# Hybrid NSA/DSA block on one core: the row factors of attention are turned as a 128x8 tile, stored to memory and read back spread over rows

## The reference

```python
z = rmsnorm(h, norm_mix) @ w_in
y_A = nsa_mixer(q_a, k, v, ...) @ w_branch_nsa     # 8 heads of 64: compressed + selected blocks + sliding window
y_B = dsa_mixer(q_b, k_b, v_b, ...) @ w_branch_dsa # 8 heads of 64: top 256 keys by an indexer
h = h + (sigmoid(g_A) * y_A + sigmoid(g_B) * y_B) @ w_out
h = h + (silu(hn @ w_gate) * (hn @ w_up)) @ w_down ; return rmsnorm(h, norm_final)
```

## Time and profile before

| | us |
|---|---|
| median of three runs (1621.24 to 1624.72) | 1623.87 |
| the profiled execution, its own time | 1621.62 |
| its span, first to last instruction | 1618.8 |
| attention stage, about | 424 to 795 |
| PE busy / DVE / ACT / POOL, of the span | 97% / 71% / 40% / 39% |

### The profile page before, as it was taken

How to read it: one execution, slowest core, us unless ns; L and a number is a source line. 1 busy time by engine, 2 the same in 40 slices (tenths; PEclk the granted TensorE clock), 3 DMA queues, 4 the chain that set the end, 5 groups by cost and what they waited for, 6 DMA issues and landing times.

```text
span 1618.8 us, 24584 instructions
## 1 busy us (share of the span) xinstructions
PE 1573.3 (97%) x9008; PEld 1328.9 (82%) x9008; DVE 1153.6 (71%) x2021; ACT 650.4 (40%) x1269; POOL 637.5 (39%) x442
## 2 busy tenths in 40 slices
PE   6999999999999989999999999999999999999997
PEld 5898888888798878898888887888888888888885
DVE  5745889999555667787675167666777776678978
ACT  5543322121565667766421144322223232344445
POOL 4233664221340144433221217444544544445454
PEclk9999999999999999999999999999999999999998
DMA  7032546321515010010254342333333335474433
GB/s 228 16 93 68 128 113 167 105 85 66 138 66 131 15 53 28 15 40 28 71 167 133 107 162 66 98 98 98 98 98 98 98 104 175 166 271 151 157 109 123
DMA packets 173303, 171.10 MB, mean 106 GB/s; under 512 B 25856, under 2 KB 126208, under 8 KB 173184
## 3 DMA queue, kind: packets, MB, share of 16 engines
q1 hardware_dynamic: 172896, 169.01, 34.5%
q10 hardware_dynamic: 288, 0.52, 0.1%
HBM read 122.04 MB, written 47.45 MB: 105 GB/s over the span
## 4 chain that ended last, share of the span: by engine, by line
PE 57%; DVE 1%; POOL 1%; DMA 0%; issue 0%; ACT 0%; SPq 0%; DVEq 0%; ACTq 0%
PE psA L1662 10%; PE psA L1664 10%; PE psA L1663 10%; PE psT L1664 6%; PE psT L1663 6%; PE psT L1662 6%; PE psT L1669 3%; PE psT L1883 3%; PE psA L1772 1%; PE psA L1773 1%; DMA s<-scratch_gates 0%; DVE merged L2418 0%; POOL h L1267 0%; POOL h L1265 0%; PE psT L1935 0%
## 5 line engine op out<-in xcount | busy, mean ns | idle before, releaser
L447 POOL TENSOR_TENSOR w_lo<-w_raw,w_hi 128x1024 fp32r<-128x1024 f32 (+2 forms) x52 | 120.3, 2315 | 257.8 <-ACT w_hi L442 257.5
L1258 POOL TENSOR_TENSOR w_lo<-w_sum,w_hi 128x1024 fp32r<-128x1024 f32 x44 | 115.4, 2625 | 119.5 <-ACT w_hi L1544 119.5
L1481 ACT ACTIVATE s<-s,nmax 128x640 f32<-128x640 f32 (+7 forms) x192 | 144.0, 752 | 29.6 <-DVE nmax L2360 27.9
L1282 POOL TENSOR_TENSOR w_lo<-act_raw,w_hi 128x512 fp32r<-128x512 f32 x77 | 107.4, 1396 | 104.7 <-ACT w_hi L1572 104.7
L1669 PE MATMUL psT<-ident,s 128*128 128x128 f32 x816 | 120.8, 278 | 0.8 <-ACT s L1481 0.8
L442 ACT CAST w_hi<-w_raw 128x1024 fp32r<-128x1024 f32 (+2 forms) x52 | 52.6, 1015 | 141.9 <-PE psA L1664 81.5
L1669 PEld LDWEIGHTS psT<-ident,s 128*128 128x128 f32 x816 | 94.4, 141 | 17.2 <-issue 7.9
L2450 DVE COPY pT<-psT 128x512 f32<-128x512 f32 (+1 forms) x116 | 69.7, 601 | 53.7 <-PE psT L1669 53.5
L2581 DVE TENSOR_TENSOR w_lo<-wd,w_hi 128x512 fp32r<-128x512 f32 x77 | 90.4, 1177 | 23.9 <-ACT w_hi L1579 23.6
L1572 ACT CAST w_hi<-act_raw 128x512 fp32r<-128x512 f32 x77 | 47.9, 622 | 123.3 <-PE psT L1664 66.4
L2250 DVE TENSOR_SCALAR_CACHE_REDUCE equal<-score,bit_try 128x512 f32<-128x512 f32 (+2 forms) x93 | 93.8, 1008 | 0.0
(11 more groups left out here) (380 smaller groups left out, 4673.7 us busy)
## 6 DMA issues: line engine op xcount, KB each, us to landing
act_raw<-scratch_act SPq DMA_DIRECT2D x77, 256.0 KB, 3.1
w_raw<-in_w_in_dram SPq DMA_DIRECT2D x24, 512.0 KB, 4.0
scratch_act<-act SPq DMA_DIRECT2D x33, 256.0 KB, 2.1
scratch_act<-act_sum SPq DMA_DIRECT2D x33, 256.0 KB, 2.1
wd<-in_w_down_dram SPq DMA_DIRECT2D x33, 256.0 KB, 3.1
scratch_gates<-gate_out SPq DMA_DIRECT2D x32, 256.0 KB, 3.1
gates<-scratch_gates SPq DMA_DIRECT2D x30, 256.0 KB, 4.1
a<-in_w_gate_dram SPq DMA_DIRECT2D x22, 256.0 KB, 3.2
```

The source lines that it names most:

```text
L447: nc.gpsimd.tensor_tensor(lo, raw, hi.bitcast(F32), ALU.subtract).then_inc(self.lo_done, 1)
L1258: nc.gpsimd.tensor_tensor(lo2[n % RING][:], block_of(n)[:], hi2[n % RING][:].bitcast(F32), ALU.subtract)\
L1282: nc.gpsimd.tensor_tensor(lo2[slot][:, 0:512], act_raw[n % 6][:], hi2[slot][:, 0:512].bitcast(F32), ALU.subtract)\
L1481: a_.activation(s_sb[v % SR][:, 0:n], s_sb[v % SR][:, 0:n], ACT.Exp, scale=-1.0, bias=nmax[:, BR[a], i, h:h + 1], accum_out=psum_p[:, BR[a ...
```

## The change

POOL no longer spreads the factors and `r_wide` is gone. DVE multiplies the 128x8 reciprocals by the gate right away (win and slc). PE turns them once at step e+4, as 128x8, to 8 partitions by 128 rows. ACT copies that to `factors_T` at step e+5, issues a store of its 4 KB to memory at e+6, waits for it at e+8, and then issues a read that lays two rows of 2 KB (even heads, odd heads) over 64 partitions each, 128x512 in all, into one of two new tiles. DVE multiplies with that tile at e+12 instead of e+7, and POOL's sum and the later steps move by five as well: `STEPS6` becomes 207, the high parts of the last NSA rows come at `len(units)+12`. In `groups6` the factors' entry comes two steps earlier and is taken out by ACT. The store and the read count on one of two semaphores, used alternately. `O_LAG` stays 6. SP is not touched.

```diff
-    R_LAG = 3
-    O_LAG, F_LAG, Y_LAG = T_LAG + 1 + V_LAG + 1, T_LAG + 1 + V_LAG + 2, 8
+    R_LAG = 4
+    O_LAG, F_LAG, Y_LAG = T_LAG + 1 + V_LAG + 1, T_LAG + 1 + V_LAG + 2 + 5, 8 + 5
...
-        if tile_of(u, O_LAG):
-            groups6.append(("r", *tile_of(u, O_LAG)))
+        if tile_of(u, R_LAG):
+            groups6.append(("r", *tile_of(u, R_LAG)))
...
-        return key[0] in ("ch", "cp") or (key[0] == "p" and key[1] % 2 == 0)
+        return key[0] in ("ch", "cp", "r") or (key[0] == "p" and key[1] % 2 == 0)
...
+    def factors_spilled(t):
+        return spilled[t % 2], spill_count(NT + 4 + t % 2) + 32 * (t // 2) + 16
+    def factors_back(t):
+        return spilled[t % 2], spill_count(NT + 4 + t % 2) + 32 * (t // 2 + 1)
...
# POOL
-            if tile_of(u, R_LAG):
-                a, i = tile_of(u, R_LAG)
...
-                if a == "dsa":
-                    nc.gpsimd.tensor_copy(r_wide[:], r).then_inc(wide_done, 1)
-                else:
...
-                    nc.gpsimd.tensor_tensor(r_wide[:], r, gate, ALU.mult).then_inc(wide_done, 1)
...
-                pool.wait_ge(t_dve, max(dve_took["r", a, i], dve_took["co", i, 0]))
+                pool.wait_ge(scaled_done, t6[a, i] + 1)
+                pool.wait_ge(t_dve, dve_took["co", i, 0])
...
# ACT
+            if tile_of(u - 2, R_LAG):
+                a, i = tile_of(u - 2, R_LAG)
+                t = t6[a, i]
+                act.wait_ge(t_act, act_took["r", a, i])
+                act.dma_start(rD[t].rearrange("r n t -> n r t"), factors_T[:]).then_inc(spilled[t % 2], 16)
+            if tile_of(u - 4, R_LAG):
+                a, i = tile_of(u - 4, R_LAG)
+                t = t6[a, i]
+                if t >= 2:
+                    act.wait_ge(scaled_done, t - 1)
+                act.wait_ge(*factors_spilled(t))
+                act.dma_start(factors[t % 2][:], rD[t].rearrange("r n t -> r (n t)").unsqueeze(1).to_broadcast([2, HD, 4 * P]))\
+                    .then_inc(spilled[t % 2], 16)
...
+            if tile_of(u - 1, R_LAG):
+                a, i = tile_of(u - 1, R_LAG)
+                act.wait_ge(t_ps, g6["r", a, i] + 1)
+                a_.copy(factors_T[:], psT[0:H, g6["r", a, i] % 3, 0:P]).then_inc(t_act, 1)
...
# PE
-            if tile_of(u, O_LAG):
...
-                turn4(group(("r", a, i)), [r_wide[:, 2 * n:2 * n + 2, :].rearrange("p a d -> p (a d)") for n in range(4)])\
-                    .then_inc(t_ps, 1)
+            if tile_of(u, R_LAG):
+                a, i = tile_of(u, R_LAG)
+                pe.wait_ge(rows_done, t6[a, i] + 1)
+                pe.transpose(group(("r", a, i))[0:H, 0:P], psum_r[:, BR[a], i, :], ident[:]).then_inc(t_ps, 1)
...
# DVE
+                branch = 1 if a == "slc" else 2
+                then(v_.reciprocal(r, psum_p[:, BR[a], i, :]))
+                v_.tensor_tensor(r, r, nsa_gate[:, i, H * branch:H * (branch + 1)], ALU.mult).then_inc(rows_done, 1)
...
-            factors = psT[:, g6["r", a, i] % 3, :]
-            dve.wait_ge(t_ps, g6["r", a, i] + 1)
+            wide = factors[t % 2][:]
+            dve.wait_ge(*factors_back(t))
```

More of the change, by code:

```diff
@@ L207, in hybrid_block @@
     yt = sb(work, "ytmp", [P, H * HD])
-    r_wide = sb(work, "row_factors_wide", [P, H, HD])
+    factors_odd = sb(work, "row_factors_odd", [P, 4 * P])
     c_st = sb(work, "c_st", [P, 4, H])
+    factors_T = sb(work, "row_factors_turned", [H, P])
     pg = sb(work, "p_group", [P, KV, 68])
@@ L219, in hybrid_block @@
     psum_r = sb(work, "psum_r", [P, 3, NT, H])
-    sb(work, "skip_merged", [P, HALF + 2 * HALF])
+    factors_even = sb(work, "row_factors_even", [P, 4 * P])
+    sb(work, "skip_merged", [P, 2 * HALF])
     c_s = sb(work, "c_s", [P, H, 64])
@@ L618, in y_ready @@
         if a == "dsa":
[L619 removed]
+            eng.wait_ge(scaled_done, t6[a, i] + 1)
         else:
@@ L650, in hybrid_block @@
     zt_ps, zt_out = sem("zt_ps"), sem("zt_out")
-    spilled = [sem(f"spilled{n}") for n in range(2)]
+    spilled = [sem(f"spilled_or_read_back{n}") for n in range(2)]
     id_ps, relu_done, sc_done = sem("id_ps"), sem("relu"), sem("score_sum")
@@ L698, in hybrid_block @@
     kD = {"slc": scratch["k_slc"], "win": scratch["k_win"]}
-    gD = scratch["gates"]
+    gD, rD = scratch["gates"], scratch["factors"]
+    factors = [factors_even, factors_odd]
+    def factors_spilled(t):
+        return spilled[t % 2], spill_count(NT + 4 + t % 2) + 32 * (t // 2) + 16
+    def factors_back(t):
+        return spilled[t % 2], spill_count(NT + 4 + t % 2) + 32 * (t // 2 + 1)
     hD, aD = scratch["h"], scratch["act"]
@@ L1194, in _ @@
                 n, r = X_AT.index(u) // 2, X_AT.index(u) % 2
-                lows, wides = sum(1 for v in range(u) if y_of(v - 1)), sum(1 for v in range(u) if tile_of(v, R_LAG))
+                lows = sum(1 for v in range(u) if y_of(v - 1))
                 if lows:
                     pool.wait_ge(yl_done, lows)
-                if wides:
-                    pool.wait_ge(wide_done, wides)
                 windows(nc.gpsimd, n, r, (cx_k, cx_v)[n])
@@ L2785 @@
         "q_nsa": (nt, P, 8 * P), "q_dsa": (nt, P, 8 * P), "k_slc": (2, 2, HD, seq), "k_win": (2, 2, HD, seq),
-        "gates": (2 * d // P, P, seq), "h": (nt, P, d),
+        "gates": (2 * d // P, P, seq), "factors": (3 * nt, 2, 4, P), "h": (nt, P, d),
         "act": (7, arrays["w_gate"].shape[2] // (2 * P), P, seq // 2)}.items()}
```

30 lines of the change are left out of this document (12 added, 18 removed).

## The result

| | us |
|---|---|
| before, median of 4 runs (1618.55 to 1624.72) | 1622.55 |
| after, median of 4 runs (1658.39 to 1667.37) | 1662.33 |
| ratio, with its 95% interval | 1.0239 [1.0214, 1.0265] |
| the profiled execution after: own time, span | 1667.37, 1665.6 |

What follows compares the result with a forecast made beforehand. PE, busy 97% of the span, was taken as the bound. Terms -7.5 - 1.3 + 0.5 (ACT) + 6 + 4 + 9.7 + 2.5 = +13.9 us on 1621.6 gave 1635.5, stated as 1637 between both bases; range 1617 to 1649.

Steps and rivals of the forecast that it cites:

- The read back over two engines: 256 KB read per tile: outermost size 2 puts it on two DMA engines, so it lands in 8.2 us.
- Rivals A and B: A: read lands in 3.1 us, 1617, chance 0.18; B: PE's lead hides all waits but the last, 1623-1625, 0.15.
- That gives PE about 2 us of lead: Attention: scores, exponentials, turnings and bank copies queued behind a standing DVE leave PE about 2 us before it stops.
- the 6 us for the DSA tiles: DSA tiles: at dsa 0 DVE stands 7 us and PE 5; dsa 1 and 2 together cost 1.
- ACT's wait for the store: 4 KB store, issued at e+6, waited for at e+8: between 0 and 0.5 us of ACT each.
- The turnings, -7.5: PE, attention: three turnings fewer per tile at 0.12 us each, the remaining one cheaper; gain 7.5 us.
- the waits for POOL, -1.3: PE's waits for POOL's spreading of the factors, 3.0 us, vanish; 1.3 us counted as gain.
- The end, +9.7: End of stage: the last read delays ACT's NSA half from 792.06 to 801.8; PE waits all 9.7 us at m_step(3).
- Both links: End of stage: merged(1), ending at 800.3, and the gates, letting DVE begin merged(2) at 805.47, stand without slack.
- The NSA tiles, +4: Waits for the read at dsa 7 and slc pass almost whole, 1.5 + 1.5 + 0.7, plus 0.3 for win: 4 us.
- The clock, +2.5 (bounds 0 and 7): Long PE waits at dsa 0 and the end lower PE's clock: 2.5 us lost, bounds 0 and 7.
- The worse case C: Two engines, read lands in 9.4 us or more, whole 5.8 us at dsa 0, clock falls repeatedly: +28, 1649; chance 0.15.

Runs made afterwards that it cites:

- the first experiment: Changed kernel with every tile's read back issued as two loads of 64 partitions each, over 16 engines: 1636.74 us, 1.0078 of before.
- the two kernels that show it bare: Before with one of four turnings per tile, 1619.77 us, 0.9970; changed kernel without store and read, sums at their old steps, 1624.61 us, 1.0004.
- no trip, old steps: Changed kernel without store and read, DVE multiplying the sums by themselves, and the sums at their old steps: 1624.61 us, 1.0004 of before.
- no trip: Changed kernel without store and read, DVE multiplying the sums by themselves, the five later steps kept: 1628.57 us, 1.0027 of before.

## Why the prediction was wrong

**The read back over two engines: right.** Its mechanism is now shown by the first experiment, and the size nearly so: 7.5 us where nothing disturbs it, 8.2 forecast. By the rule of the Trainium skill (DMA: Bandwidth & Descriptors, "Why a DMA increments its semaphore by 16 and not by 1") it was two engines, and the trace agrees: a DMA share of 0.13 and two small packets, where the two DMAs with 64 outermost have 32. Rivals A and B fall.

**"That gives PE about 2 us of lead": the step that failed first.** On it rested the 6 us for the DSA tiles, of which 1 for dsa 1 and 2. Measured: 20 us. At dsa 0 PE does stop 2.2 us less than DVE (7.70 for 9.86), but behind it next to no lead is left. DVE's stops of 2.20 and 2.88 us at dsa 1 and 2 are followed by PE stops of 2.01 and 2.60, and so on:

```profile
465.64 0.69 DVE L2402 TENSOR_TENSOR ya<-row_factors_odd,acc 128x512 f32<-128x512 f32 x1 [2.20 <-DMA row_factors_odd<-scratch_factors]
...
479.89 0.69 DVE L2402 TENSOR_TENSOR ya<-row_factors_even,acc 128x512 f32<-128x512 f32 x1 [2.88 <-DMA row_factors_even<-scratch_factors]
```
```profile
467.33 0.44 PE L1897 MATMUL psT<-pT,v_b 128*64 128x128 f32 x4 [2.01 <-DVE pT L2469]
...
481.98 0.66 PE L1897 MATMUL psT<-pT,v_b 128*64 128x128 f32 x8 [2.60 <-DVE pT L2469]
```

Four score banks look like slack, but behind the product stand also DVE's copies of the turned probabilities, which PE needs in the same step. These two reads took 9.4 and 9.6 us from issue to product, more than 8.2. DVE's stops for reads of DSA tiles come to 20.4 us together, and 20 is what these reads cost: here, in sum, a stop of DVE is a stop of PE. In the NSA tiles 11.0 us of stops cost 6. For dsa 0 itself the term (7 for DVE, 5 for PE) was near what its read cost, 6.7; the other seven DSA tiles cost 13, not 1. (A tile's cost is not its own alone: without the trip of dsa 0 the next tiles lost 5.3 us more.) What the loads add to the landing at dsa 0 was taken at half of 5.8 us; 13.0 against 7.5 is 5.5, nearly the whole. By the Trainium skill (DMA: Bandwidth & Descriptors, "Queues, rings and completion order") each engine takes turns between the queues. The trace agrees for the transfer itself: from 444 to 447 it ran at 25 KB a us, alone at 50, and took 8.2 us in place of 5.8. That is 2.5 of the 5.5 us. The other 3.0 passed before the first packet, which came 4.3 us after the issue and not 1.3; so that the sum comes near the whole 5.8 is chance.

**ACT's wait for the store, "between 0 and 0.5 us of ACT each" and no term in the sum: failed.** It was priced from 64 KB stores on a quiet stretch although showed the engines full. It is 6 us by the run without a store. ACT stops at the two places where SP loads in bulk; that the stop costs the program anything is seen at dsa 0 alone (3 us by the run without that trip, 5.4 from dsa 0 to dsa 2 without stores), not at dsa 5.

**The key loads at dsa 5: missed.** The trace of before had them, and the read and store there run into them. ACT stops 5.46, PE 2.68 and 5.44 us. From the reciprocal of dsa 5 to that of dsa 6 it takes 30.9 us now (524.54 to 555.39), before 22.4.

**The turnings, -7.5, and the waits for POOL, -1.3: right for PE's work, wrong for the time.** (Its own terms, 8.6 - 24 x 0.06, give 7.2.) PE's busy time fell by 7.0 and 7.9 us in the two kernels that show it bare. Only 4.9 us reach the time in the kernel of before, and none in the changed order, though there the waits for POOL are gone too: 1.0004, where these terms had -8.8 us. PE at 98 to 99.8% was read as "work taken off PE there comes back in full"; PE waits for DVE's copies instead.

**The end, +9.7: too large.** The 9.9 of the profile are luck, since 4.1 of them lie behind `m_step(5)`. Counted from the last reciprocal, `m_step(3)` starts 4.8 us later than before, `m_step(4)` and `m_step(5)` 5.8. ACT's copies of the NSA half came 6.9 us later and not 9.7: the read was issued 2.2 us earlier than forecast (the queue does not wait for the copies ahead of it to run), and it landed in 7.5 us and not 8.2. Then DVE took 2.2 us less for the low parts (before, then after):

```profile
793.65 4.70 DVE L2397 TENSOR_TENSOR yTl_nsa<-y_raw_nsa,yTh_nsa 128x512 fp32r<-128x512 f32 x4
```
```profile
836.48 2.50 DVE L2416 TENSOR_TENSOR yTl_nsa<-y_raw_nsa,yTh_nsa 128x512 fp32r<-128x512 f32 x4 [2.11 <-ACT yTh_nsa L1433]
```

The 5 us between landings of 8.2 and 3.1 are 0.7: with the last tile's read over 16 engines the gates' chain binds. Both links were said to "stand without slack", and then only one of them was costed. The five later steps alone lose 3.5 us there, so the whole trip adds some 2.

**The NSA tiles, +4:** 6 by ratio for sixteen tiles and the end, the last of them worth next to nothing. The term has 1.5, 1.5 and 0.7 for stops of 3.2, 2.7 and 1.3 us that were to "pass through almost whole". The first is less the old wait of 1.74; the other two are half, without a reason given, and half is what the runs show.

**The clock, +2.5 (bounds 0 and 7): too small.** The changed kernel and that without trip and with old steps have the same 8936 PE instructions; PE is busy for 1579.7 and 1565.4 us, 14.3 more. The mean granted clock is 0.981 against 0.994, at 0.88 and 0.93 in the stretches after the long waits. In the attention stage alone it is 12.1 us, at 0.94 and 0.99 (after, then without the trip):

```profile
424.00:855.90 431.90, 380.23 (x3468) 331.71 (x3469) 268.19 (x702) 252.75 (x620) 113.72 (x132) 0.94 0.25 69
```
```profile
424.00:814.00 390.00, 368.13 (x3458) 321.33 (x3459) 267.04 (x692) 250.91 (x615) 114.06 (x132) 0.99 0.22 59
```

Some of it would have been idle time anyway, so it isn't all loss; how much was not separated.

Together, by the ratios along a chain of kernels:

| step | forecast, us | measured, us |
|---|---|---|
| before to "no trip, old steps": turnings, POOL's spreading | -8.8 | 0.6 |
| to "no trip": five steps later | 4.6 | 3.7 |
| to "all over 16": store, wait and read | 0.5 | 8.3 |
| to after: two engines in place of 16 | 15.1 | 26.1 |
| the clock (measured: within the other rows) | 2.5 | |
| sum | 13.9 | 38.8 |

The forecast's terms are those of the prediction; 4.6 is its end with a landing in 3.1 us, and 15.1 is 6 + 4 + 5.1. Three rows are wrong by 8 to 11 us each, all on the same side. The measured rows are uncertain by 2 to 5 us, as their intervals go. The worse case C had 3 us more at dsa 0, 5 at other tiles and a lower clock, and ended at 1649: it kept the lead, the free store and the turnings' gain, so its bound was none.

## What to carry to other kernels

Before a transfer is put between two engines in lock step, look at its outermost size, and at what is in flight on the same DMA engines when it starts: the 4 KB store here was held 6 and 8.7 us by the bulk loads ahead of it. Split the broadcast read by destination partition (two DMAs here, 26 us). And price a wait inserted in an engine's list at its full length unless the list behind it is shown to have slack; a busy share doesn't show that, only the timeline of what the next engine takes does.

## What was not expected of the hardware

ACT's issues of small DMAs take longer than the 0.37 us of the earlier trace rows, 0.61 us for the store (1.18 at dsa 0) and 0.54 for the read:

```profile
L1440 ACTq DMA_DIRECT2D scratch_factors<-row_factors_turned x24: 613/614/1183, 434.1 to 822.6; - x24
```

They run beside the ACT instructions ahead of them: the copies that start at 826.20 stand before the read of 826.14 in ACT's list. What stands behind them waits: in twelve tiles the next ACT instruction is the copy to `acc`, and it starts 0.04 to 0.10 us after the end of the store's issue. So the issue is not free for what stands behind it.

A small DMA beside bulk loads is late before its first packet. In 22 tiles the store's first packet comes 1.27 us (1.26 to 1.29) after its issue and its last ends 0.13 us later. With SP's 2 MB loads in flight the first came after 4.3 us (dsa 0), with the key loads after 6.7 (dsa 5), and ACT got past its wait 6 and 8.7 us after the issue. The reads of these two tiles had their first packets after 4.3 and 7.3 us, 1.3 in the quiet. Over 16 engines, at the same place, the product of dsa 0 still followed its issue at 438.36 by 6.8 us. What holds the packets back for so long no run here shows.
